# Loading x already transposed, and its row norms by a product with ones, at the head of a two-layer float32 kernel

## The reference

```python
def rms_norm(x, gain):
    x32 = x.astype(jnp.float32)
    y = x32 * lax.rsqrt(jnp.mean(x32 * x32, axis=-1, keepdims=True) + NORM_EPS)
    return (y * gain.astype(jnp.float32)).astype(x.dtype)
...
    h = rms_norm(x, mix_norm_gain)
    proj = jnp.einsum('bsd,de->bse', h, w_in)
...
    x = x + jnp.einsum('bsd,de->bse', merged, w_out)
```

## Time and profile before

| | |
|---|---|
| median of 3 runs | 1045.61 us (1045.43 to 1045.82) |
| the profiled execution, its own time | 1044.29 us |
| its span | 1042.4 us |
| TensorE busy | 922.1 us, 88% |
| VectorE busy | 478.0 us, 46% |
| ScalarE busy | 238.5 us, 23% |
| moved by DMA | 289.05 MB, mean 277 GB/s |

### The profile page before, as it was taken

The page is one execution under the profiler, slowest core; times in us unless marked ns, Lnnn a source line. Parts: engine busy times, 40 slices in busy tenths (PEclk is TensorE's granted clock), DMA queues, the critical chain, the costliest instruction groups (busy, mean ns, idle before and its releaser), DMA issues.

```text
span 1042.4 us, 19452 instructions
## 1 busy us (share of the span) xinstructions
PE 922.1 (88%) x8320; PEld 612.6 (59%) x8320; DVE 478.0 (46%) x1087; ACT 238.5 (23%) x498; POOL 4.7 (0%) x11
## 2 busy tenths in 40 slices
PE   9999999999999999999999998876667766677686
PEld 7986467764489999644696465543333433343343
DVE  4894546678685555567668442211111101111032
ACT  2015223361221111000412052321122122221123
POOL 0100000000000000000000000000000000000000
PEclk9999999999999999999999999988888888888888
DMA  9744320035254444753256799999999999999995
GB/s 372 291 173 173 141 103 2 2 129 206 103 203 162 162 162 163 284 199 122 81 199 287 296 398 429 431 425 434 431 427 428 434 433 431 428 429 433 433 425 230
DMA packets 23849, 289.05 MB, mean 277 GB/s; under 512 B 2801, under 2 KB 4593, under 8 KB 9457
## 3 DMA queue, kind: packets, MB, share of 16 engines
q1 hardware_dynamic: 23792, 288.23, 67.6%
HBM read 287.17 MB, written 1.05 MB: 276 GB/s over the span
## 4 chain that ended last, share of the span: by engine, by line
PE 68%; DMA 27%; DVE 4%; issue 1%; ACT 1%; SPq 0%; ACTq 0%; DVEq 0%
DMA sb_ring<-w_exp 26%; PE ps L1281 12%; PE ps L469 9%; PE ps L869 6%; PE ps L1319 6%; PE ps L814 5%; PE ps L1378 2%; PE ps L1197 2%; PE ps L1437 2%; PE ps L796 1%; PE ps L826 1%; PE ps L858 1%; PE ps L1267 1%; PE ps L1357 1%; PE ps L1156 1%; PE ps L489 1%
## 5 line engine op out<-in xcount | busy, mean ns | idle before, releaser
L469 PE MATMUL ps<-sb_ring,sb_own 128*32 128x256 f32 x1936 | 155.8, 484 | 103.1 <-DMA sb_ring<-w_exp 99.9
L469 PEld LDWEIGHTS ps<-sb_ring,sb_own 128*32 128x32 f32 x1936 | 75.6, 138 | 180.3 <-DMA sb_ring<-w_exp 110.5
L2914 DVE TENSOR_TENSOR sb_own<-sb_own,ps 128x128 f32<-128x128 f32 x32 | 9.2, 288 | 336.6 <-ACT sb_own L1962 336.6
L1281 PE MATMUL ps<-sb_nsa,sb_ring 128*128 128x128 f32 x640 | 74.7, 275 | 0.0
L1281 PEld LDWEIGHTS ps<-sb_nsa,sb_ring 128*128 128x128 f32 x640 | 73.1, 192 | 0.0
L1973 ACT ACTIVATE sb_own<-ps 128x256 f32<-128x256 f32 x32 | 12.3, 385 | 208.0 <-PE ps L469 208.0
L489 PE MATMUL ps<-sb_ring,sb_own 128*32 128x256 f32 (+1 forms) x992 | 58.0, 375 | 1.6 <-DVE sb_own L2914 1.0
L1281 PE MATMUL ps<-sb_hT,sb_ring 128*128 128x128 f32 x480 | 56.9, 275 | 0.0
L1281 PEld LDWEIGHTS ps<-sb_hT,sb_ring 128*128 128x128 f32 x480 | 55.3, 192 | 0.1
L814 PE MATMUL ps<-sb_ring,sb_hT 128*128 128x512 f32 (+1 forms) x128 | 50.6, 550 | 0.0
L489 PEld LDWEIGHTS ps<-sb_ring,sb_own 128*32 128x32 f32 x992 | 29.5, 109 | 26.4 <-issue 10.8
(11 more groups left out here) (621 smaller groups left out, 1462.7 us busy)
## 6 DMA issues: line engine op xcount, KB each, us to landing
sb_ring<-w_exp SPq DMA_DIRECT2D x26, 4096.0 KB, 23.6
sb_ring<-w_exp SPq DMA_DIRECT2D x35, 2048.0 KB, 22.9
sb_ring<-w_in SPq DMA_DIRECT2D x13, 2048.0 KB, 8.2
sb_ring<-w_gu SPq DMA_DIRECT2D x11, 2048.0 KB, 7.9
sb_ring<-w_dn SPq DMA_DIRECT2D x10, 1024.0 KB, 6.8
sb_ring<-w_out SPq DMA_DIRECT2D x4, 2048.0 KB, 7.8
sb_ring<-w_exp SPq DMA_DIRECT2D x10, 512.0 KB, 8.6
sb_ring<-w_branch SPq DMA_DIRECT2D x2, 2048.0 KB, 8.7
```

Source lines behind the costliest of these rows:

```text
L469: m = pe.matmul(ps[group(j), 2, 0:256], hgT[:, k, :], w[j // 2][k][:, (j % 2) * 256:(j % 2 + 1) * 256], start=(k == 0), stop=(k == KT - 1))
L1281: m = pe.matmul(out[:, i, :], w[:, k, i * P:(i + 1) * P], h[:, k, :], start=start and i == 0 and k == 0, stop=(k == KT // 2 - 1), skip_gro ...
```

## The change

The host hands over `xT` as well: x with features on the partitions, as eight tiles of 128 features by 256 tokens. It is loaded in three parts (two, two and four tiles: 256, 256 and 512 KB), each just ahead of the part of the first weight block that goes with it, and behind `cols`. The transposes, their PSUM banks and the load of `x` in rows at the head are gone; `x` in rows is loaded once TensorE has made the row sums, behind `w_in` 3 and ahead of `w_in` 4, and the place where it is added to waits for it. ScalarE squares `xT` in three parts into the space of `x`; VectorE folds the eight tiles of squares into one by three additions; TensorE multiplies a matrix of ones with it, after the first column tile of the third part, which gives all partitions the 256 row sums; ScalarE takes the root of these, and VectorE the reciprocal of 128x256 values. The two sums of block 1 that VectorE made before `hT` come after the sums on `hT`.

```diff
+        x_ones, x_wide = merge[:, 0, 1, 0:P], merge[:, 0, 0, 0:T]
+        xT = merge[:, 1].rearrange("p i (k t) -> p (i k) t", t=T)
+        X_PARTS = (slice(0, 2), slice(2, 4), slice(4, KT))
+        squared_x = x.rearrange("p b n -> p (b n)")
...
         def _(sp):
-            sp.dma_start(x.rearrange("p b n -> p (b n)"), dram["x"].rearrange("p b n -> p (b n)")).then_inc(sig("x_loaded"), 16)
             sp.dma_start(cols, dram["cols"]).then_inc(sig("cols_loaded"), 16)
+            def load_xT(part):
+                ks = X_PARTS[part]
+                sp.dma_start(xT[:, ks].rearrange("p k t -> p (k t)"), dram["xT"][:, ks].rearrange("p k t -> p (k t)")).then_inc(sig(f"xT{part}_loaded"), 16)
...
+                if n == 4:
+                    sp.wait_ge(sig("x_widened"), since("x_widened", 1))
+                    sp.dma_start(x.rearrange("p b n -> p (b n)"), dram["x"].rearrange("p b n -> p (b n)")).then_inc(sig("x_loaded"), 16)
                 if n >= 4:
                     wait_used(sp, stream[n - 4])
...
                     for q in range(2):
+                        load_xT(q)
                         sp.dma_start(dst[:, q * 1024:(q + 1) * 1024], dram["w_in"][0][:, 2 * q:2 * q + 2].rearrange("p k n -> p (k n)"))\
                           .then_inc(sig(f"w_in0_{q}_loaded"), 16)
+                    load_xT(2)
...
         def _(pool):
+            pool.memset(x_ones, 1.0).then_inc(sig("ones_ready"), 1)
...
-            pe.wait_ge(sig("x_loaded"), 16)
             pe.wait_ge(sig("cols_loaded"), 16)
-            for half in range(2):
-                for b in range(NB):
-                    transposes(2 * b + half, [x[:, b, (4 * half + n) * P:(4 * half + n + 1) * P] for n in range(4)], "x_turned")
-
             w = ring[:, 0, :].rearrange("p (k n) -> p k n", n=BANK)
             for part, tiles in enumerate((range(0, 2), range(2, 4), range(4, KT))):
+                pe.wait_ge(sig("h_ready"), since("h_ready", part + 1))
                 if part < 2:
-                    pe.wait_ge(sig("h_ready"), since("h_ready", 2))
                     pe.wait_ge(sig(f"w_in0_{part}_loaded"), 16)
                 else:
-                    pe.wait_ge(sig("h_ready"), since("h_ready", 4))
-                    pe.wait_ge(sig("x_spread"), since("x_spread", 1))
-                    for b in range(NB):
-                        m = pe.matmul(ps[:, 6, b * P:(b + 1) * P], x_spread[:, b, :], ident, start=True, stop=True)
-                    m.then_inc(sig("x_widened"), 1)
                     arrived(pe, ("w_in", 0))
                 for ct in range(4):
+                    if part == 2 and ct == 1:
+                        pe.wait_ge(sig("ones_ready"), 1)
+                        pe.wait_ge(sig("x_summed"), 1)
+                        pe.matmul(ps[:, 6, 0:T], x_ones, squared_x[:, 0:T], start=True, stop=True).then_inc(sig("x_widened"), 1)
...
-            act.wait_ge(sig("x_loaded"), 16)
-            for b in range(NB):
-                act.activation(merge[:, b, 1, :], x[:, b, :], ACT.Square, accum_out=stat[:, b:b + 1]).then_inc(sig("x_squared"), 1)
-            act.wait_ge(sig("x_squared"), since("x_squared", NB))
+            for part, ks in enumerate(X_PARTS):
+                act.wait_ge(sig(f"xT{part}_loaded"), 16)
+                act.activation(squared_x[:, ks.start * T:ks.stop * T], xT[:, ks].rearrange("p k t -> p (k t)"), ACT.Square).then_inc(sig("x_squared"), 1)
             act.wait_ge(sig("cols_loaded"), 16)
-            act.activation(stat[:, 0:NB], stat[:, 0:NB], ACT.Sqrt, bias=cols[:, C_EPS:C_EPS + 1], scale=1.0 / D).then_inc(sig("x_root"), 1)
             act.wait_ge(sig("x_widened"), since("x_widened", 1))
-            act.activation(x_wide, ps[:, 6, 0:T], ACT.Copy).then_inc(sig("x_wide_ready"), 1)
+            act.activation(x_wide, ps[:, 6, 0:T], ACT.Sqrt, bias=cols[:, C_EPS:C_EPS + 1], scale=1.0 / D).then_inc(sig("x_root"), 1)
...
+            def h_out(part):
+
+                ks = X_PARTS[part]
+                dve.wait_ge(sig(f"xT{part}_loaded"), 16)
+                dve.tensor_tensor(h_raw[:, ks, :], xT[:, ks, :], spread(cols[:, C_MIX + ks.start:C_MIX + ks.stop], 2, T), ALU.mult)\
+                   .then_inc(sig("h_ready"), 1)
...
-            for n in range(4):
-                h_out(n)
+            for part in range(3):
+                h_out(part)
+            dve.wait_ge(sig("x_squared"), since("x_squared", 3))
+            for n in (1024, 512):
+                link(dve.tensor_tensor(squared_x[:, 0:n], squared_x[:, 0:n], squared_x[:, n:2 * n], ALU.add))
+            dve.tensor_tensor(squared_x[:, 0:T], squared_x[:, 0:T], squared_x[:, T:2 * T], ALU.add).then_inc(sig("x_summed"), 1)
             dve.wait_ge(sig("x_root"), since("x_root", 1))
-            link(dve.reciprocal(stat[:, 0:NB], stat[:, 0:NB]))
-            dve.tensor_copy(x_spread, spread(stat[:, 0:NB], 2, P)).then_inc(sig("x_spread"), 1)
+            link(dve.reciprocal(x_wide, x_wide))
...
-            arrived(dve, ("w_in", 1))
-            link(left_sums(in_sums[1], first_block, 0))
-            link(left_sums(in_sums[1], first_block, 1))
-            dve.wait_ge(sig("x_wide_ready"), since("x_wide_ready", 1))
-            dve.wait_ge(sig("h_ready"), since("h_ready", 4))
+            dve.wait_ge(sig("h_ready"), since("h_ready", 3))
...
             link(right_sums(h_right, h_block, 3))
-            left_sums(in_sums[1], first_block, 2).then_inc(sig("in_sums_ready"), 2)
+            arrived(dve, ("w_in", 1))
+            link(left_sums(in_sums[1], first_block, 0))
+            left_sums(in_sums[1], first_block, 1).then_inc(sig("in_sums_ready"), 1)
+            left_sums(in_sums[1], first_block, 2).then_inc(sig("in_sums_ready"), 1)
+            dve.wait_ge(sig("in_sums_ready"), since("in_sums_ready", 1))
             left_sums(in_sums[1], first_block, 3).then_inc(sig("in_sums_ready"), 1)
...
                     dve.wait_ge(sig("w_out_copied"), since("w_out_copied", 1))
+                    dve.wait_ge(sig("x_loaded"), 16)
```

More of the change, by code:

```diff
@@ L94 @@
     "branch_vector": [("oa_sums_ready", 1), ("branch_sums_ready", 3), ("branch_summed", 5), ("w_out_sums_ready", 3), ("m_sums_ready", 1)],
-    "delta_vector": [("warm_ready", 1), ("x_spread", 1), ("h_scaled", 1), ("conv_ready", 1), ("y_ready", 1), ("norms_inverse", 1), ("norms_read", 1), ("g_spread", 2), ("gc_read", 1), ("roped", 1), ("kb_ready", 1), ("gc_out", 1),
+    "delta_vector": [("warm_ready", 1), ("h_scaled", 1), ("conv_ready", 1), ("y_ready", 1), ("norms_inverse", 1), ("norms_read", 1), ("g_spread", 2), ("gc_read", 1), ("roped", 1), ("kb_ready", 1), ("gc_out", 1),
         ("a_ready", 1), ("qk_ready", 1), ("kd_ready", 1), ("o_mean", 1), ("o_normed", 1), ("x2_spread", 1), ("h2_scaled", 1)],
-    "delta_scalar": [("x_squared", 2), ("x_root", 1), ("x_wide_ready", 1), ("qk_squared", 1), ("norms_ready", 1), ("softplus_ready", 1), ("g_ready", 1), ("exp_gc_ready", 1), ("decays_ready", 1), ("o_copied", 1), ("o_squared", 1), ("x2_squared", 2), ("x2_wide_ready", 1)],
+    "delta_scalar": [("x_squared", 3), ("x_root", 1), ("qk_squared", 1), ("norms_ready", 1), ("softplus_ready", 1), ("g_ready", 1), ("exp_gc_ready", 1), ("decays_ready", 1), ("o_copied", 1), ("o_squared", 1), ("x2_squared", 2), ("x2_wide_ready", 1)],
     "delta_tensor": [("x_widened", 1), ("qk_summed", 1), ("norms_spread", 1), ("gc_ready", 1), ("g_widened", 1), ("kk_ready", 1), ("kv_turned", 2), ("x2_widened", 1)],
     "rows_normed": [("x2_summed", 4)],
-    "rows_turned": [("x_turned", 4), ("merge_turned", 4), ("x2_turned", 4), ("x3_turned", 4), ("x4_turned", 4)],
-    "rows_ready": [("h_ready", 4), ("h2_ready", 4), ("h3_ready", 4), ("h4_ready", 2)],
+    "rows_turned": [("merge_turned", 4), ("x2_turned", 4), ("x3_turned", 4), ("x4_turned", 4)],
+    "rows_ready": [("h_ready", 3), ("h2_ready", 4), ("h3_ready", 4), ("h4_ready", 2)],
     "ffn_tensor": [("qkv_projected", 2), ("block_made", 35), ("projected", 10), ("plain_made", 2), ("product_made", 7 * (N_FC - 1)), ("down_made", N_FC - 1), ("last_product", 7)],
@@ L2027, in turned_out @@
                        .then_inc(sig(signal_out), 1)
-            def h_out(n):
-                half, b = n // 2, n % 2
-                dve.wait_ge(sig("x_turned"), since("x_turned", n + 1))
-                dve.tensor_tensor(h_raw[:, 4 * half:4 * half + 4, b * P:(b + 1) * P], ps[:, 2 * b + half, :].rearrange("p (k t) -> p k t", t=P),
-                                  spread(cols[:, C_MIX + 4 * half:C_MIX + 4 * half + 4], 2, P), ALU.mult).then_inc(sig("h_ready"), 1)
+            def h_out(part):
[3 more added lines that the diff above has]
+                   .then_inc(sig("h_ready"), 1)
             dve.memset(zeros, 0.0).then_inc(sig("warm_ready"), 1)
             dve.wait_ge(sig("cols_loaded"), 16)
-            for n in range(4):
-                h_out(n)
+            for part in range(3):
[4 more added lines that the diff above has]
```

(5 more changed lines are left out.)

1 line of the change is left out of this document (removed).

## The result

| | before | after |
|---|---|---|
| median of 22 runs each | 1045.08 us (1044.03 to 1045.95) | 1046.41 us (1045.41 to 1047.72) |
| ratio after : before | | 1.0015 [1.0009, 1.0021] |
| profiled execution: time, span | 1044.29, 1042.4 us | 1046.35, 1044.5 us |

By the ratio the change costs about 1.6 us (0.9 to 2.2), by the medians 1.3. That is clear of the noise, but under the 0.2% by which this document calls a kernel slower. The forecast was no change, 1045.7 us in 1044.2 to 1047.6. Single executions of one kernel lie up to 2.3 us apart. The spans of the two profiled executions differ by 2.1 us; the one of before was 0.8 us faster than the median of its kernel, the one of after lies on its own.

A forecast was written before the change was run, and what follows sets the result against it. TensorE bounds the kernel after the head, so block 1's end decides; VectorE's waits give back TensorE's 2.5 us, leaving +0.1 us: 1044.4 against 1044.29, plus 1.32 to the runs' median, forecast 1045.7 us, range 1044.2 to 1047.6.

The forecast's parts named there:

- the prediction's own signs of being wrong: First block starting after 8 us, TensorE's two waits absent, or rows after 36 us shifted by more than 2 us.
- The start of the first block: TensorE's first products start at 6.0 us, bounds 5.97 and 7.9, with 978 KB landed at about 5.6.
- The rule weighed against it: Head of the DMA queue: about 2.0 us fixed cost per transfer besides bytes, putting the first block's start at 9.0 us.
- Rival 2: Head of the queue: each small transfer pays 2.5 us, first block starts at 10.6; +4.7 us, 1050.3; chance 0.05.
- The first block: TensorE: product with ones at 14.7 us, folds and squares hidden with 1.9 us to spare, end at 20.4 against 22.85.
- The table load: ScalarE, ahead of the root: hidden in the wait for row sums and costs nothing; if not, 1.28 us are added.
- rival 3: ScalarE: the root's table load is not hidden, or the root waits for something else; +1.3 us, 1047.0; chance 0.07.
- VectorE's path: Root 0.48, reciprocal 1.75, hT 2.36 us: hT ready at 20.05, block 1's first sums at 25.45, L2167's result at 31.85.
- TensorE's waits: Block 1: TensorE waits for VectorE twice, 1.5 us for the first sums and 1.05 us for L2167's result.
- The sum: End of block 1 at 35.45 us against 35.36 before, +0.1 us: TensorE's 2.5 us gain is given back in waits.
- Rival 1: Block 1: VectorE does not hold it and TensorE's gain is kept, end at 32.9; -2.5 us, 1043.1; chance 0.05.
- Rival 4: TensorE's clock falls in its two new waits; at 1.2 GHz five products cost 8.9 us more; chance 0.02.

The follow-up runs named there:

- e6: Kernel before the change, with x loaded in four transfers of 256 KB in place of one of 1024 KB: 1045.88 us, ratio 1.0010 to before.
- e5: Changed kernel with all of xT in one 1024 KB transfer, first in the queue ahead of cols: 1046.9 us, ratio 1.0021 to before.
- e2: Changed kernel with the first two parts of xT loaded as one 512 KB transfer: 1047.92 us, ratio 1.0025 to before.
- e1: Changed kernel with ScalarE's wait for cols moved ahead of the squares: 1045.11 us, ratio 1.0000 to before.
- e3: Changed kernel with the reciprocal taken of 2 of the 256 columns only, leaving out part of the norm: 1044.44 us, ratio 0.9993 to before.
- e7: Changed kernel with ScalarE's cols wait moved ahead of the squares and VectorE's block 1 work in order of need: 1042.58 us, ratio 0.9975 to before.
- e4: Changed kernel with sums 0 and 1 of block 1 moved from VectorE to GpSimd: 1048.82 us, ratio 1.0037 to before.
- e8: Changed kernel with VectorE's block 1 work in order of need, ScalarE's cols wait left in place: 1044.03 us, ratio 0.9993 to before.

## Why the prediction was right, and which terms were not

The forecast of the time held: no change by the bound of 0.2%, inside the range. Its working was right in the main mechanism and wrong in two terms of the sum. One of the prediction's own signs of being wrong came true: rows after 36 us are shifted by 2.62 us, and it had set 2.

- **The start of the first block** was set at P = 6.0, from the landings of before by bytes: "978 KB should be there at about 5.6". It was 7.23, since that quarter landed at 7.1: the term was short by 1.2 us, with the measured value inside its bounds, 5.97 and 7.9. The step that failed is that a landing depends on bytes alone. e6 shows that the same bytes in pieces of 256 KB come 1.1 us later, e5 that one transfer of 1024 KB brings the landings of before back, e2 something between.
- **The rule weighed against it** gave 9.0 for P, and that was not right either. The first four landings, at 3.2, 5.2, 7.1 and 9.1 us, are 1.9 to 2.0 us apart whether 256 or 512 KB lie between. The page "DMA: Bandwidth & Descriptors" of the Trainium skill, in its section on the anatomy of one DMA, has 2.0 us for each transfer and its bytes on top, so 2.6 and 3.2 us as an estimate. The section gives this for transfers issued by GpSimd, which the prediction left out; these are issued by SyncE. The trace agrees with neither of these, and lies between that rule and the bytes alone.
- **Rival 2** (small transfers late, from P = 8.0 on) did not come about in after, whose P stopped 0.8 us short of it. A part of its mechanism is there, since cutting costs 1.1 us in e6, but not the 2.5 us for each transfer that it was priced at.
- **The first block** took P to 16.06 for the product with ones, P + 8.83 against the P + 8.7 forecast; folds and squares ended at 15.2, before it. Right, but closer than forecast: they were set at 12.8, with 1.9 us to spare, and had 0.9, because part 2 of `xT` landed at 11.65 and not at 9.2.
- **The table load** was costed at nothing; it is 1.28 us on the path. This is rival 3, given 0.07, and e1 shows it: moving one wait takes 1.19 us off the last addition. The row on which the step rested has a load in front of one wait; the root had two. The diff showed both waits, so this could have been seen.
- **VectorE's path** was right: root 0.47 (0.48), reciprocal 1.75 (1.75), `hT` 2.36 (2.36). The first sums were ready at 28.0, P + 20.8; the forecast of P + 19.45 with the table load is P + 20.7. L2175's result came at 34.2, P + 27.0; the forecast with the load is P + 27.1. e3 shows that this path sets the time.
- **TensorE's waits** were forecast as two of 1.5 and 1.05 us. There were three, 1.00, 1.40 and 0.66: the load made `hT` late as well. In e1, without it, they are two, 1.29 and 0.72. So `hT` was ready at 22.7 and not at 20.05, and the hole ahead of the last addition was 0.60 us, where almost none was forecast.
- **The sum.** With the two measured terms, P + 29.45 + 1.28 - 35.36 is 7.23 - 4.63 = +2.60; the profile has +2.62. The step from there to the later stages, "moves that stage too, by as much", held at 2.2 us in the chain and 2.1 in the spans, and the medians differ by 1.3.
- **Rival 1** (TensorE's gain is kept) could not hold with VectorE's order as it is. e7 shows what it takes: the load hidden and the sums in the order of need.
- **Rival 4** (the clock falls in the waits for VectorE) did not happen in after, whose granted clock was 1.00 from 4 to 40 us and whose records of block 1 have the length that they had before. It did happen in e4, behind a wait for VectorE of 4.11 us, and in e5 behind another pause, in the head.

That the forecast held owes something to luck. Both mis-sized terms had the same sign, 1.2 and 1.3 us, and the shift of 2.6 us by the profile is above 0.2%; by the times it is 1.6 (0.9 to 2.2). The base helped too: the forecast stood on a median of 3 runs, 1045.61, and that of 22 is 1045.08, so a forecast of +0.1 us on a base that was 0.5 us high came within 0.7 us of a result that is 1.3 above the later median. And the lower end of the range does not follow from its rule: a third of the 2.6 us between the sum and rival 1 gives 1044.8, not 1044.2. The result lies above both.

Not settled: why small pieces at the head of the queue are slow. In e6, 1746 KB in six transfers landed at 9.15, in after the same amount in five transfers at 10.4, so the number of transfers alone does not order them. Nor why P is 6.79 to 7.42 between after, e1, e3, e4, e7 and e8, whose queues are the same up to there: VectorE starts on part 0 of `xT` at 4.49 in e3 and at 5.54 in e7. Part of it is the warm-up, which ends at 6.9 in e3 and 5.9 in e8.

## What to carry to other kernels

A gain on the engine that bounds a stage is worth only what its supplier keeps up with: list what that supplier does in order, and put it in the order of need before or with the change, since here the change alone lost 1.6 us and with the order and one moved wait won 2.6 (both by the ratio to before). Where a row of the trace stands for an operation, compare what stands ahead of it in the code too: a table load was free behind one wait and cost its 1.28 us behind two. At the head of a program, take the landing of a piece from transfers cut as that piece is, not from the bytes landed by larger ones.

## What the runs showed of the hardware

- **The table load** (1.28 us) ran 4 us before its activation when the activation had one wait in front (e1: load 12.82, root 16.78), and after the last one when it had two (after, e8: load 16.74 and 16.57, right behind the product; e1, squares: load 5.28, where it ran at 0.71 behind one wait).
- **Pieces at the head of the queue:** 1234 KB were in by 6.3 us as 1024 + 210 KB, 7.4 with the 1024 KB in four, 7.8 in three transfers of 210 and 512 KB, 9.1 in four of 210 to 512 KB.
- **The clock:** behind a pause of 1.91 us after 4.84 us of warm-up (e5) came some 3 us at 1.2 GHz, and the 40 products around them took 10.56 us in place of 8.87. The same came behind a pause of 4.11 us in e4, where 32 products took 5.43 us in place of 3.81, and behind one of 2.37 us at 643.8 us of e5. Each time the products had gone on at 2.4 GHz for some 1 us before the fall. Pauses of 0.72 to 1.29 us behind the warm-up (after, e1, e2, e6, e7, e8) left 2.4 GHz, and so did one of 2.82 us at 638 us of before. What decides it is open. The page "TensorE: Matmul & The Clock Gate" of the Trainium skill, in its section "Why this matters for your kernels", asks one to keep the gaps between bursts of products short; e4 and e5 agree in kind, the pause at 638 us does not.
- **GpSimd and VectorE** hold each other up: two VectorE instructions of 128x1024 took 5.46 us in place of 2.36 beside two of GpSimd. The first ran from 20.26 to 22.45, while GpSimd's first ended at 21.36; the second from 22.37 to 25.72, while GpSimd's second ended at 24.64. Both VectorE instructions end 1.1 us after GpSimd's, which is about what one of them takes alone. The Trainium skill's page "SBUF — State Buffer", in its section on who interferes with whom, has the two engines share a pair of ports that one of them holds at a time, which bears on a VectorE instruction with two inputs in SBUF beside a GpSimd one that reads SBUF, as here; the trace agrees with its times.
